# Moving branch A's projection out of its own stage and into attention, in pieces of 512 columns

## The reference

```python
h = rms_norm(x, norm_in)
u_a, v_a, z_a, q_b, k_b, v_b, z_b, gate_a, gate_b = split(h @ w_in)       # nine times 1024 columns
# branch A: chunks of 128 tokens, 8 channel groups
v_a = rms_norm(gelu(v_a), norm_v)
y_a = gelu(u_a) * (tril(w_s) @ v_a + b_s) * silu(z_a)
# branch B: 8 heads of 128, strictly causal
logits = q @ k.T / sqrt(128)
w[t, s] = sigmoid(logits[t, s]) * prod(1 - sigmoid(logits[t, j]) for s < j < t)
y_b = (w @ v) * silu(z_b)
merged = sigmoid(gate_a) * (y_a @ w_o_gmlp) + sigmoid(gate_b) * (y_b @ w_o_sb)
out = rms_norm(x + merged @ w_out, norm_final)
```

## Time and profile before

| | |
|---|---|
| time, median of 3 runs | 2738.89 us (2737.4 to 2738.95) |
| the profiled execution | 2739.31 us, span 2737.6 us |
| TensorE (PE) busy | 2586.8 us, 94% |
| VectorE (DVE) busy | 1597.0 us, 58% |
| ScalarE (ACT) busy | 1260.3 us, 46% |
| GpSimd (POOL) busy | 928.9 us, 34% |
| TensorE's mean granted clock | 0.97 |
| DMA | 283.57 MB, mean 104 GB/s |

### The profile page before, as it was taken

How to read it: one execution, slowest core, us unless ns; L and a number is a source line. 1 busy time by engine, 2 the same in 40 slices (tenths; PEclk the granted TensorE clock), 3 DMA queues, 4 the chain that set the end, 5 groups by cost and what they waited for, 6 DMA issues and landing times. The chain is left out here.

```text
span 2737.6 us, 38907 instructions
## 1 busy us (share of the span) xinstructions
PE 2586.8 (94%) x13812; PEld 2224.3 (81%) x13812; DVE 1597.0 (58%) x2057; ACT 1260.3 (46%) x2212; POOL 928.9 (34%) x776
## 2 busy tenths in 40 slices
PE   6999999999989999999995999799999999799998
PEld 5788888888768888888885999688777778689997
DVE  7555554545655455555543444689888899534342
ACT  5564333443445433343432221588888878411111
POOL 2434232332444333232321221366666665000000
PEclk8999999999999999999996999999999999899999
DMA  3333333333222323333336444111221122443331
GB/s 101 107 96 127 105 114 117 98 118 101 95 69 88 105 99 119 101 117 114 101 104 192 134 136 154 70 61 68 77 77 46 73 77 77 139 153 111 121 122 62
DMA packets 239712, 283.57 MB, mean 104 GB/s; under 512 B 12048, under 2 KB 189200, under 8 KB 236560
## 3 DMA queue, kind: packets, MB, share of 16 engines
q1 hardware_dynamic: 229008, 265.86, 30.1%
q10 hardware_dynamic: 10624, 16.78, 1.7%
HBM read 190.32 MB, written 92.27 MB: 103 GB/s over the span
## 5 line engine op out<-in xcount | busy, mean ns | idle before, releaser
L720 PE MATMUL in_bank<-in_a_hi,in_w_hi 128*128 128x512 f32 x1988 | 778.3, 392 | 26.5 <-ACT in_o L425 16.8
L722 PE MATMUL in_bank<-in_a_lo,in_w_hi 128*128 128x512 f32 x1988 | 775.5, 390 | 0.0
L723 PE MATMUL in_bank<-in_a_hi,in_w_lo 128*128 128x512 f32 x1988 | 775.4, 390 | 0.0
L720 PEld LDWEIGHTS in_bank<-in_a_hi,in_w_hi 128*128 128x128 f32 x1988 | 374.6, 188 | 107.0 <-ACT in_o L425 17.7
L723 PEld LDWEIGHTS in_bank<-in_a_hi,in_w_lo 128*128 128x128 f32 x1988 | 374.4, 188 | 78.2
L722 PEld LDWEIGHTS in_bank<-in_a_lo,in_w_hi 128*128 128x128 f32 x1988 | 374.8, 189 | 77.3
L407 ACT ACTIVATE in_w_hi<-in_sums 128x512 fp32r<-128x512 f32 x284 | 179.0, 631 | 474.4 <-PE in_bank L723 325.4
L563 DVE TENSOR_TENSOR in_w_lo<-carried_buffer,in_w_hi 128x512 fp32r<-128x512 f32 x213 | 242.0, 1136 | 260.8 <-ACT in_w_hi L407 257.8
L1571 DVE TENSOR_TENSOR_SCAN att_rest<-att_z_ps,att_rest 128x512 f32<-128x512 f32 (+3 forms) x320 | 355.5, 1117 | 47.6 <-ACT att_z_ps L1520 44.8
L1478 POOL TENSOR_TENSOR att_slot<-att_slot,att_rest 128x512 f32<-128x512 f32 (+3 forms) x320 | 305.0, 958 | 216.0 <-DVE att_rest L1571 215.5
L303 POOL TENSOR_TENSOR in_sums<-carried_buffer 128x512 f32<-128x512 f32 x71 | 91.7, 1292 | 698.8 <-DMA carried_buffer<-in_w_in 696.8
(11 more groups left out here) (169 smaller groups left out, 4776.9 us busy)
## 6 DMA issues: line engine op xcount, KB each, us to landing
carried_buffer<-in_w_in SPq DMA_DIRECT2D x144, 512.0 KB, 4.8
uz_T<-in_o SPq DMA_DIRECT2D x32, 256.0 KB, 4.6
va_T<-in_o SPq DMA_DIRECT2D x32, 256.0 KB, 3.5
q_T<-in_o SPq DMA_DIRECT2D x32, 256.0 KB, 3.6
k_T<-in_o SPq DMA_DIRECT2D x32, 256.0 KB, 3.5
vb_T<-in_o SPq DMA_DIRECT2D x32, 256.0 KB, 3.6
zb_T<-in_o SPq DMA_DIRECT2D x32, 256.0 KB, 3.5
ga_T<-in_o SPq DMA_DIRECT2D x32, 256.0 KB, 3.6
```

The source lines that it names most:

```text
L720: pe.matmul(bank[:, :], hi, a_hi[:, i, k], start=opens and k == 0, stop=False, skip_group_check=True)
L722: pe.matmul(bank[:, :], hi, a_lo[:, i, k], start=False, stop=False, skip_group_check=True)
L723: mm = pe.matmul(bank[:, :], lo, a_hi[:, i, k], start=False, stop=k == HALF_K - 1, skip_group_check=True)
```

## The change

The second stage becomes `gate_and_mix`: the same tile by tile work up to y_a, which is now stored unsplit to a new DRAM tensor `ya_T`; no projection, no split of y_a or w_o_gmlp there. v_ps and m_ps have two PSUM tiles each, v_a and uz four input buffers, y three. All loops are written out.

The third stage takes the projection as filler. Logits are now made in units of 512 queries by 512 keys (four pieces), from the last queries to the first and from the nearest keys to the farthest, ten units a head, so only ten slot buffers are needed. Each piece is one slot of a common list; `B` follows six slots after its piece (`LAG`), `P` two after that (`BEHIND`). From slot 14 on, 256 filler pieces `F` (three matmuls of 512 columns each) are spread evenly over 328 slots; eight make one block of pa_T (128 channels by 512 tokens), which VectorE multiplies with its gate (`G`). Two passes of four output blocks go over the tokens, so each tile of ya_T is loaded and split twice. q, k, v, ya and w_o_gmlp all come as items of 512 columns through eight raw buffers. `f_ps` and `y_ps` have one PSUM bank each. All low parts (`K`) but those of v and of the weights are made by GpSimd.

```diff
-def gate_and_project_a(nc, norm_v, w_s, b_s, w_o_gmlp, s, carried):
+def gate_and_mix(nc, norm_v, w_s, b_s, s):
...
+        v_ps = [sc.ps(f"v_ps{n}", [P, D]) for n in range(2)]
+        m_ps = [sc.ps(f"m_ps{n}", [P, D]) for n in range(2)]
...
 # VectorE
+            gain_mix(0)
+            for t in range(NT):
+                if t + 2 < NT:
+                    mean(t + 2)
+                if t + 1 < NT:
+                    gain_mix(t + 1)
+                times_uz(t)
+                if t + 2 < NT:
+                    rest_v(t + 2)
...
 # TensorE
+            def turn(t):
+                pe.wait_ge(va_loaded[t % IN_BUFS], 16 * (t // IN_BUFS + 1))
+                if t >= 2:
+                    pe.wait_ge(v_lo_done, t - 1)
...
+            def mix(t):
+                pe.wait_ge(v_lo_done, t + 1)
+                if t >= 2:
+                    pe.wait_ge(gained, t - 1)
...
+            for t in range(NT):
+                mix(t)
+                if t + 2 < NT:
+                    turn(t + 2)
```

```diff
+SLOTS = 10
+W_BUFS = 4
+RAWS = 8
+LAG = 6
+BEHIND = 2
+F_FIRST = 14
...
+        self.units = [(h, sup, g) for h in range(HEADS) for sup in reversed(range(NSUP)) for g in reversed(range(sup + 1))]
+        self.pieces = [(h, sup, g, r) for h, sup, g in self.units for r in range(QT)]
...
+                wanted.append((max(free_k, need - 5, -1), ("k", h, sup)))
+                wanted.append((max(free_v, need + 2), ("v", h, sup)))
+                wanted.append((max(free_q, start[h, sup, sup] - 6, -1), ("q", h, sup)))
+        n_slots = len(self.pieces) + LAG + BEHIND
+        fills, n_fills = {}, HEADS * QT * KT
+        slot_of = [F_FIRST + f * (n_slots - F_FIRST) // n_fills for f in range(n_fills)]
...
+        for h in range(HEADS):
+            for j in range(KT):
+                wanted.append((slot_of[(QT * h - 1) * KT + j] + 1 if h else j, ("a", h, j)))
...
+        for slot in range(n_slots):
+            if slot < len(self.pieces):
+                order.append(("Z", slot))
+            order += at.pop(slot, [])
+            if 0 <= slot - LAG < len(self.turns):
+                order.append(("B", slot - LAG))
+            for f in fills.get(slot, []):
+                order.append(("F", f))
+                if f % KT == KT - 1:
+                    order.append(("G", f // KT))
+            m = slot - LAG - BEHIND
+            if 0 <= m < len(self.turns):
+                order.append(("P", m))
+                h, sup, g, kt = self.turns[m]
+                if kt == QT - 1 and g == 0:
+                    order.append(("Y", h * NSUP + NSUP - 1 - sup))
...
+        y_ps, f_ps = sc.ps("y_ps", [P, CW]), sc.ps("f_ps", [P, CW])
...
 # VectorE
+            def gated_block(i):
+                dve.wait_ge(f_read, KT * (i + 1))
+                dve.wait_ge(gate_loaded[i % 2], 16 * (i // 2 + 1))
+                dve.tensor_tensor(gate[i % 2][:, :], f_ps[:, :], gate[i % 2][:, :], ALU.mult).then_inc(f_done, 1)
...
 # TensorE
+            def project_a(f):
+                i, j = divmod(f, KT)
+                h, r = divmod(i, QT)
+                if j == 0:
+                    wait_past(pe, f_done, i)
+                cols = slice(r * P, (r + 1) * P)
+                tokens, weights = ("a", h, j), ("w", h // NSUP * QT + r, j // (KT // 2))
+                pe.wait_ge(split_done, max(split_of[tokens], split_of[weights]) + 1)
+                pe.matmul(f_ps[:, :], wo_hi[:, j, cols], ya_hi[:, j], start=j == 0, stop=False)
+                pe.matmul(f_ps[:, :], wo_hi[:, j, cols], ya_lo[:, j], start=False, stop=False)
+                pe.matmul(f_ps[:, :], wo_lo[:, j, cols], ya_hi[:, j], start=False, stop=j == KT - 1).then_inc(f_read, 1)
```

More of the change, by code:

```diff
@@ L875, in gate_and_project_a @@
[L875 to L890 removed]
+        va_loaded, uz_loaded = sc.sems("va_loaded", IN_BUFS), sc.sems("uz_loaded", IN_BUFS)
@@ L892, in _ @@
+        turned, squared, mean_done, rms_done, v_hi_done, v_lo_done, mixed, gained, biased, y_done = (
+            sc.sem(n) for n in ("turned", "squared", "mean_done", "rms_done", "v_hi_done", "v_lo_done", "mixed",
+                                "gained", "biased", "y_done"))
+        stored = sc.sems("stored", Y_BUFS)
+        block = memory.enter_context(nc.Block())
         @block.sync
         def _(sp):
[L894 to L902, removed]
@@ L1225, in z_pieces @@
-def z_pieces(sup):
-    return [("Z", i, at, min(ZW, (i + 1) * P - at)) for i in range(sup * QT, (sup + 1) * QT)
-            for at in reversed(range(0, (i + 1) * P, ZW))]
-def b_steps(sup):
-    wide, narrow = list(range(1, QT * sup + 1)), list(reversed(range(QT * sup + 1, QT * (sup + 1))))
-    order = [0]
-    while wide or narrow:
-        order += [tiles.pop(0) for tiles in (narrow, wide) if tiles]
-    return [("B", sup, kt) for kt in order]
-def with_splits(logits, splits, at):
-    out = list(logits)
-    for split, place in reversed(list(zip(splits, at))):
-        out.insert(place, split)
-    return out
@@ L1320, in attention @@
+def attention(nc, w_o_gmlp, w_o_sb, s, carried):
+    w = Pieces()
+    BLOCKS = HEADS * QT
     with ExitStack() as memory:
@@ L1395, in quarter @@
[L1395 to L1416 removed]
+        raw_loaded = sc.sems("raw_loaded", RAWS)
@@ L1544, in _, with split @@
-            for part in range(len(SPLITS)):
-                split_qk(0, part)
-            act.wait_ge(ones_set, RESTS)
-            for n, e in enumerate(early):
-                sigmoids(*e[1:], 0, n)
-            per_head(act, body)
+            def split(item):
+                which, m, n = item
+                src, loaded, count = raw_of(item)
+                act.wait_ge(loaded, count)
+                if which in "qk" and m:
+                    act.wait_ge(z_full, w.last_logits((which, m - 1, n)) + 1)
+                elif which == "a" and m:
+                    act.wait_ge(f_read, (QT * m - 1) * KT + n + 1)
+                elif which == "w" and m >= QT:
+                    act.wait_ge(f_read, (BLOCKS // 2 - QT + m % QT + 1) * KT)
+                act.activation(halves(item)[0], src, ACT.Copy).then_inc(split_hi, 1)
```

949 lines of the change are left out of this document (389 added, 560 removed).

## The result

| | before | after |
|---|---|---|
| median, us | 2738.9 (2737.4 to 2740.9, 4 runs) | 2803.6 (2800.4 to 2806.0, 4 runs) |
| ratio to before, 95% interval | 1 | 1.0231 [1.0219, 1.0243] |
| profiled execution, span, us | 2737.6 | 2801.2 |
| attention begins | 1734.8 | 1614.2 |
| last y multiply of attention begins | 2348.1 | 2406.4 |

A forecast was written before the change was run, and what follows sets the result against it. TensorE was to bound attention, after a serial mixing loop at half clock. Last y multiply: 1620.3 + 710.4 + 15 + 40 + 4 = 2389.7, 41.6 later; 2739.3 + 41.6 + 5 = 2786 us, own range 2762 to 2805.

The forecast's parts named there:

- The likeliest case: Whole kernel: slower, 2786 us against 2739.3 for the profiled execution before; chance 0.45.
- TensorE's need: Attention: TensorE needs 66.7 + 22.1 = 88.8 us a head, 710 for eight, and becomes the bound.
- The mixing stage: Branch A without its projection: serial loop, period 9.05 us at clock 0.50; attention begins at 1617.0, 118 us saved.
- Rival 1: Mixing stage: full clock, periods of 6.5 us, attention begins 42 us earlier than forecast, 2744 us in all; chance 0.12.
- One bank each for F and Y: Attention: TensorE waits for VectorE's late multiplies, 17 us for F and 23 for Y, together 40, bounds 0 to 60.
- Rival 2: Attention: no waits for the single banks since VectorE might be early, 2786 - 40 = 2746 us; chance 0.15.
- rival 3: Both stages: mixing at full clock and TensorE never held by a bank, 2786 - 42 - 40 = 2704 us; chance 0.10.
- The start of attention: First 18 slots: GpSimd's 44 us of splits and weight products against TensorE's 29, 15 us lost, bounds 5 and 25.
- Bunched splits: Attention: eight y_a splits within ten slots load GpSimd with 25 us against TensorE's 22; 4 us lost, 0 to 20.
- The way out: Into the output stage: roundings wait for the third piece of w_o_sb, now loaded only at the very end; +5 us.
- Rival 4: Attention: small waits in each slot also cost the clock, 3.75 us a head, 30 in all, 2816 us; chance 0.18.
- The gain on offer: Attention: idle and low clock at the turn of heads should go, 8.3 us a head, 66 in all.

The follow-up runs named there:

- mix_reorder: Changed kernel with VectorE's rest of v(t+2) put before the gain multiply of t+1 in the mixing loop: 2780.3 us.
- mix_filler: Changed kernel with eight extra 512-column matmuls on constant operands, results overwritten, ahead of each tile's mix: 2770.5 us.
- mix_rms: Changed kernel with mix_reorder's VectorE order, and GpSimd's power of tile t+2 ahead of the bias add of tile t: 2766.3 us.
- best1: Changed kernel with mix_rms and y2f2 joined, and the first two pieces of w_o_sb rounded without waiting for the third: 2728.3 us.
- f_gap: Changed kernel with at least one slot without a filler piece behind each block of eight F pieces, same banks: 2783.9 us.
- y2_z2: Changed kernel with two PSUM banks for Y and two instead of three for logits: 2778.4 us.
- y2f2: Changed kernel with two PSUM banks each for Y, F, logits and transposes: 2766.9 us.
- ramp_vec: Changed kernel with the low parts of the first eight pieces each of y_a and w_o_gmlp made by VectorE instead of GpSimd: 2804.4 us.
- old_a_new_att: Changed kernel with branch A and its projection as before the change, attention in the new order without filler, one Y bank: 2790.7 us.
- old_a_new_att_y2: old_a_new_att with a second PSUM bank for Y in place of the unused F bank: 2713.3 us, 0.9905 of the kernel before.
- best3: best1 with four 512-column filler matmuls ahead of each tile's mix: 2712.6 us, 0.9910 of the kernel before.

## Why the prediction was right, and where its sizes were off

The likeliest case came true in its three main mechanisms: the serial mixing loop at half clock, the waits on the two single banks, and TensorE as the bound of attention. The time is 17.6 us above the 2786 forecast and inside its own range (2762 to 2805), if near its upper end. Two of its signs did not come out: a head takes 97 us, not near 94, and the start lost its time only in part to GpSimd.

- *TensorE's need.* 88.8 us a head by 0.23 us for 512 columns. The pace is 0.2333 (2060.70, 2060.94, 2061.17, 2061.40, 2061.63 are successive starts), so the term of 710 is 717: 7 us of the excess.
- *The mixing stage.* Period 9.05 forecast, 9.03 measured; clock 0.50 forecast, 0.51; attention at 1617.0, measured 1614.15. It came 2.9 earlier though the bias add takes 3.26 instead of 2.5, which only the last tile feels. mix_reorder shows that the loop lay in VectorE's order. What the text left out is the second loop right behind it, through GpSimd: at 7.44 it took away a part of the gain that the cure for the first would have had.
- *The clock.* Rival 1 (full clock, 2744) is out for this kernel. Its price was 42 us; mix_filler bought 33 with the added matmuls in it. The Trainium skill (TensorE: Matmul & The Clock Gate, Part 1, "What's actually happening") has sustained activity release the clock. mix_rms disagrees with the plain reading: TensorE busy 80.00 us of 80 and the clock at 0.50. What it is in mix_filler that raised the clock these runs don't tell. best1 has the same mixing loop as mix_rms and 0.69 to 0.84 in the windows shown; but its profile is its fastest execution and that of mix_rms its slowest, and both kernels spread over some 15 us from execution to execution, and their mean clock with it (0.963 to 0.971 in mix_rms, 0.962 to 0.971 in best1). So the two profiles don't show that the kernels differ there.
- *One bank each for F and Y.* 40 forecast by idle times. The rows show 24.8 + 16.8 = 41.6, so the rows to come were forecast well. Their price was the term that was mis-sized. What attention took, less the other terms, leaves 2406.4 - 1618.5 - 717 - 17.5 = 53, and by the one wait read above each costs 0.24 more than its row has: 41.6 + 46 x 0.24 = 53. Counted over all 46 it is 51.1. Rival 2 (2746) is out, as f_gap, y2_z2 and y2f2 show, and with it rival 3 (2704), which needed both this and rival 1. The waits were 27 and 19 with up to 1.7 us, for 31 each of 0.4 to 1.2 forecast. Here lie 11 to 13 us of the excess.
- *The start of attention.* 15 forecast. First load to first logits are 3.5 us; head 0 is some 14 us longer than its smaller work would make it, which is worked out and not shown by a run. Here the size was right and the cause only in part. Behind the first logits, TensorE's waits up to 1665 sum to 8.2 us, and of these only 4.0 are for GpSimd (3.7 for weights, 0.2 for a key split); 2.3 are for VectorE and 2.0 for loads of v. Most of the rest is the clock, which the term had left out: 0.80 over the first 51 us, and 0.87 from 1624 to 1664, some 10 us at half pace, which cost 5 (an estimate). That the size came out near 15 is partly luck. ramp_vec moved the load and not the time. How the 70 us of this term and the one above divide stays open by a few us.
- *Bunched splits.* 4 us forecast. Behind the first slots TensorE waits for no split, and once, at 2044.78, 0.98 us for weights which GpSimd made late behind a row of splits of y_a, q and w_o_gmlp. The loads, 3.3 forecast, took 4.3.
- *The way out.* +5 forecast, 19.50 - 14.45 = 5.05.
- *Rival 4* (the small waits bring the clock down) is out: 46 waits on Y and F, and clock 1.00 in every window of a head from 1665 to 2370. What the Trainium skill (TensorE: Matmul & The Clock Gate, "A second HAM failure mode: psum-queue depth-cycling") says of small idles that make the clock oscillate isn't borne out by them. But the longer waits of old_a_new_att, up to 2.5 us, came with 0.94 to 0.96, and the second bank with 1.00. And the prediction read the trace of before too smoothly when it found a low clock only where TensorE idled for 4 us. From 1745 to 1768 there TensorE waited twelve times for VectorE, 0.28 to 0.72 us each and never longer, and this window in between shows 0.83:

```profile
1755.00:1765.00 10.00, 8.35 (x28) 5.56 (x29) 8.40 (x9) 7.80 (x18) 7.34 (x9) 0.83 0.00 0
```

So small waits that stand close together may cost clock, which no run tries; those on Y and F, some 6 a head, did not.

In the sum, with the upper figure for the waits: +7 (pace), +13 (waits), +2.5 (start), +1 (loads), -2.9 (earlier), -4 (splits): 16.6 of 17.6.

The gain on offer, 66 us from the idle turn of heads and its low clock, was there in part: the 4 us waits are gone and the clock is 1.00. But the runs show that it belongs to attention's new order, not to the projection that was moved: old_a_new_att_y2, which has the one and not the other, is 26 us faster than before, and behind its first logits it has no wait on a split of q or k. (The new order is units, slots and early splits together; no run takes these apart.) Its heads take 71.0 us instead of 75.0, so 4 of the 8.3 us a head were had, with VectorE busy 76.25 of 80; what holds the rest wasn't tried. The move itself takes filler from a stage that was bound by TensorE without a gap and gives it to one that no longer has a gap to fill. With everything mended (best3, 2712.6) it comes out no faster than without the move (2713.3), though best3 also has the earlier rounding of w_o_sb, worth some 3 us in best1, which the other lacks, and other banks. Unmended it costs 12.9 us (old_a_new_att against after).

## What to carry to other kernels

Before work is moved away as filler, look at what it covered: a stage that was full at the high clock (60.00 busy of 60 at 1.00) became a loop of one tile at a time at the low one, in which an engine's order that ties tile t+2 to tile t costs time, and so does the clock. A second PSUM bank for an accumulator that one late instruction reads was worth more here than a third bank for a stream (25 us for Y against the logits' third): count when the reading engine gets to that instruction in its own order, and expect each wait to cost more than its row shows, here by 0.2 us. Undo a two-part change by halves: here one half with one more bank was as fast as the whole with everything mended, with far less to mend. And where executions of one kernel spread over some 15 us, ask which of them was profiled before two profiles are compared.

## What the runs showed of the hardware

- Added work can buy time through the clock: 128 matmuls of 512 columns whose result is thrown away made the kernel 33 us faster, the granted clock of the stage going from 0.51 to 0.84 to 1.00.
- A TensorE without a gap is no sign of the full clock: 100 us at 80.00 of 80 and 20.00 of 20 stayed at 0.50 in the profiled execution of mix_rms. The same kernel took 2756 to 2771 us, with mean clocks from 0.971 down to 0.963.
- GpSimd's 128x1024 bias add takes 2.36 us, but 3.26 when VectorE's uz multiply of the same shape runs beside it (after, mix_reorder, mix_filler: both start within 0.2 us), and again 2.36 when only VectorE's a_v_lo pass, which reads PSUM, falls beside it (mix_rms). In the last two tiles of that same run the uz multiply falls beside it, and it takes 3.27 and 3.25. That the uz multiply is the cause wasn't tried by itself.
- Two Y banks gave 77.4 us for 64.4 us of waits. Start to start the waits come to 71.9; the rest came with the clock (0.94 to 0.96, then 1.00).
